# Attention over pairs of heads: two 64-row rotary products in neighbouring PSUM banks, and the causal mask added by VectorE

## The chip, the cores and the metric

The kernel runs on one core of a Trainium2 chip. Its time is the device time of one execution in microseconds (us); the figure to compare is the median over several executions. A profile of one execution, with a record for nearly every instruction, goes with it.

## The reference, cut to what matters

A two-layer decoder trunk over 512 tokens of width 1024, in float32. Layer 0 has a state-space and a gated linear recurrence mixer, layer 1 has multi-head latent attention, and each layer ends in a mixture of experts (64 experts). The change lies in the attention of layer 1 alone:

```
q, k: 8 heads of 192 = 128 ("nope") + 64 (rotary); v: 8 heads of 128
for each block of 128 queries:
    s = einsum('bhqd,bhkd->bhqk', q_blk, k) / sqrt(192)
    s = where(key_pos <= q_pos, s, -1e30)
    p = softmax(s)
    o = einsum('bhqk,bhkd->bhqd', p, v)
x = x + concat(o) @ w_o
```

## The kernel before, in words

The core has five engines with an instruction stream each: TensorE (PE), VectorE (DVE), ScalarE (ACT), GpSimd (POOL) and SyncE (SP), which only issues transfers. Each stream is executed in the order in which the program wrote it; streams wait for each other by semaphores, and nothing but the waits in the code orders them.

The attention (`odd_tensor`, `odd_scalar`, `odd_vector`) goes over 32 units, numbered n = 8c + i: query block c of 4, head i of 8. The kernel is causal, so a unit of block c meets only (c + 1) * 128 keys. Below k stands for c + 1, the number of 128-key pieces, 1 to 4. `ps` is the accumulator memory PSUM, eight banks of 512 float32 per partition. For one unit:

- PE, "QK": `qTn` by `kTn`, 128 rows deep (L923), then the mask added by a product of the identity with the mask matrix on the last 128 columns (L924), then the rotary part `qTr` by `kTr`, 64 rows deep (L925). The rotary parts of two heads lie over one another in the partitions: even heads in partitions 0 to 63, odd heads in 64 to 127. The product ends with an increment of `s_sc`. Scores of unit n go to bank n % 3.
- VectorE: row maximum of the scores (L1094), its multiple as bias (L1097, which increments `s_mx`).
- ScalarE: exponential out of PSUM into `pr` with the row sum (L1016, `s_ex`).
- VectorE: reciprocal of the sum (L1102) and scaling of `pr` (L1104, `s_pn`).
- PE: k transposes of `pr` into banks 3 and 4 (L933, `s_pt`).
- ScalarE: copy of these into `pT` (L1024, `s_pte`).
- PE, "AV": k products of V with `pT` into bank 5 or 6 (L943, `s_o`). After four heads VectorE copies the bank to `oT` (L1109, `s_oe`).

The order on each engine is written out by hand as a software pipeline. PE: QK of n, transposes of n - 2, AV of n - 3. VectorE: maximum and bias of n, then reciprocal and scaling of n - 1. ScalarE: exponential of n, then the copy of n - 2:

```python
for n in range(NHD + 3):          # PE;  NHD = 32
    ...QK(n)...
    m = n - 2
    if 0 <= m < NHD:
        TE.wait_ge(s_pn, m + 1)   # the scaled probabilities of unit m
    ...
for n in range(H * TC + 5):       # VectorE
    if n < H * TC:
        V.wait_ge(s_sc, n + 1)
        vlink(V.reduce_max(...n...)) ...
    m = n - 1
    if 0 <= m < H * TC:
        V.wait_ge(s_ex, m + 1) ... .then_inc(s_pn, 1)
```

`vlink` makes VectorE wait for its own instruction before the next one. Each float32 matmul is recorded as two PE instructions, called passes here; a transpose is one.

Ahead of the attention come the projections and the normalisation of q and k, behind it the output projection (`outproj_tensor`, L441), which waits for the last `oT` copy, then the norm, the routing and the experts. SP waits for `s_sc` of the last unit (L1819) before it loads the first expert weights of layer 1 into the buffers that held q and k.

Of the kernel before, what the change touches and what calls it, by code (L numbers as in the profile page):

```python
# [8 lines left out]
ALU = mybir.AluOpType  # L9
ACT = mybir.ActivationFunctionType  # L10
AX = mybir.AxisListType

P = 128
# [9 lines left out]
H = 8  # L23
QL, KVL, NOPE, ROPE, VD = 384, 256, 128, 64, 128
QK = NOPE + ROPE
MLA_IN = QL + KVL + ROPE
ATT_SCALE = 1.0 / math.sqrt(QK)
# [45 lines left out]
def hybrid_decoder(nc, a, out):  # L73
    ctx = ExitStack()
    with ctx:
# [14 lines left out]
        extra = sb("extra", [P, 4096])  # L90
# [5 lines left out]
        ps = ctx.enter_context(nc.psum_tensor("ps", [P, 8, 512], F32))  # L96

        ident = con[:, C_ID:C_ID + P]
# [3 lines left out]
        mask = con[:, C_MASK:C_MASK + P]  # L102
# [18 lines left out]
        r3 = ring[3][:, :, :].rearrange("p a b -> p (a b)")  # L121
# [25 lines left out]
        def vlink(ins):  # L147
            chain["v"] += 1
            ins.then_inc(s_v, 1)
            nc.vector.wait_ge(s_v, chain["v"])  # L150
# [11 lines left out]
        V, S, G, TE = nc.vector, nc.scalar, nc.gpsimd, nc.tensor  # L162
# [377 lines left out]
        def tt(o, p, q, op):  # L540
            vlink(V.tensor_tensor(o, p, q, op))  # L541
# [251 lines left out]
        vbuf = rega[:, :].rearrange("p (c n) -> p c n", c=TC)  # L793
# [12 lines left out]
        rp = [r[:, 2560:3584].rearrange("p (h d) -> p h d", h=2 * H) for r in rows]  # L806
        sq = extra[:, 0:1536]
        cbuf = extra[:, 1536:1536 + MLA_IN]
        pr = [r3[:, 4096:4608], extra[:, 2240:2752], r3[:, 4608:5120]]
        pT = [extra[:, 2752:3264], extra[:, 3264:3776]]  # L810
        kro = extra[:, 3776:4032].rearrange("p (c d) -> p c d", c=TC)
        half = ROPE // 2
        rt = [sq[:, i * 512:(i + 1) * 512].rearrange("p (h d) -> p h d", h=2 * H) for i in range(3)]
# [52 lines left out]
        def odd_tensor():  # L866
            for n in range(2):
                for c in range(TC):
                    if c == 0:
                        TE.wait_ge(s_win, 32)  # L870
                    for k in range(KC):
                        last = TE.matmul(ps[:, 4 * n + c, 0:HW], hT[:, k, c * P:(c + 1) * P], win[n][:, k, :],  # L872
                                         start=k == 0, stop=k == KC - 1)
                    last.then_inc((s_ch, s_c)[n], 1)
                    if n and c:
                        odd_ctrans(c - 1)
            odd_ctrans(TC - 1)
            for u, (kind, c, n) in enumerate(UNITS):
                if u == 0:
                    TE.wait_ge(s_uq, 16)  # L880
                    TE.wait_ge(s_cte, TC)
                if u == 3:
                    TE.wait_ge(s_ukv, 16)
                if u >= 8:
                    TE.wait_ge(*copied(u - 8))
                bank = ps[:, u % 8, :]
                cc = slice(c * P, (c + 1) * P)
                if kind == "q":
                    for k in range(3):
                        last = TE.matmul(bank, cT[:, k, cc], wuq[:, k, n * 512:(n + 1) * 512],  # L890
                                         start=k == 0, stop=k == 2)
                elif kind == "kv":
                    for k in range(2):
                        last = TE.matmul(bank, cT[:, 3 + k, cc], wukv[:, k, n * 512:(n + 1) * 512],
                                         start=k == 0, stop=k == 1)
                else:
                    if n == 0:
                        TE.wait_ge(s_qn, c + 1)
                    for j in range(4):
                        if n < 2:  # L900
                            src = qi[c % 2][:, 4 * n + j, 0:NOPE]
                        elif n < 4:
                            src = ki[c % 2][:, 4 * (n - 2) + j, :]
                        else:
                            src = rp[c % 2][:, 8 * (n - 4) + 2 * j:8 * (n - 4) + 2 * j + 2, :]\
                                .rearrange("p h d -> p (h d)")
                        last = TE.transpose(bank[:, j * P:(j + 1) * P], src, ident)
                last.then_inc(s_q, 1)
            for u in range(len(UNITS) - 8, len(UNITS)):
                TE.wait_ge(*copied(u))  # L910


            NHD = H * TC
            for n in range(NHD + 3):
                if n < NHD:
                    c, i = n // H, n % H
                    nk = (c + 1) * P
                    if n >= 3:
                        TE.wait_ge(s_ex, n - 2)
                    r = slice(64 * (i % 2), 64 * (i % 2) + 64)  # L920
                    cc = slice(c * P, (c + 1) * P)
                    o = ps[:, n % 3, 0:nk]
                    TE.matmul(o, qTn[:, i, cc], kTn[:, i, 0:nk], start=True, stop=False)  # L923
                    TE.matmul(ps[:, n % 3, nk - P:nk], ident, mask, start=False, stop=False)  # L924
                    TE.matmul(o, qTr[r, i // 2, cc], kTr[r, i // 2, 0:nk], start=False, stop=True)\  # L925
                        .then_inc(s_sc, 1)
                m = n - 2
                if 0 <= m < NHD:
                    TE.wait_ge(s_pn, m + 1)
                    if m >= 2:  # L930
                        TE.wait_ge(s_pte, m - 1)
                    for b in range(m // H + 1):
                        last = TE.transpose(ps[:, 3 + m % 2, b * P:(b + 1) * P],  # L933
                                            pr[m % 3][:, b * P:(b + 1) * P], ident)
                    last.then_inc(s_pt, 1)
                m = n - 3
                if 0 <= m < NHD:
                    c, i = m // H, m % H
                    if m % 4 == 0 and m >= 8:
                        TE.wait_ge(s_oe, m // 4 - 1)  # L940
                    TE.wait_ge(s_pte, m + 1)
                    for b in range(c + 1):
                        last = TE.matmul(ps[:, 5 + (m // 4) % 2, (m % 4) * P:(m % 4 + 1) * P],  # L943
                                         vbuf[:, b, i * VD:(i + 1) * VD],
                                         pT[m % 2][:, b * P:(b + 1) * P], start=b == 0, stop=b == c)
                    last.then_inc(s_o, 1)
            TE.wait_ge(s_oe, 2 * TC)
            outproj_tensor(lambda k, c: oT[:, k, c * P:(c + 1) * P])

# [7 lines left out]
        def odd_scalar():  # L957
# [52 lines left out]
            for n in range(H * TC + 2):  # L1010
                if n < H * TC:
                    nk = (n // H + 1) * P
                    S.wait_ge(s_mx, n + 1)
                    if n >= 3:
                        S.wait_ge(s_pt, n - 2)
                    S.activation(pr[n % 3][:, 0:nk], ps[:, n % 3, 0:nk], ACT.Exp, scale=ATT_SCALE,  # L1016
                                 bias=nb[:, n % 3:n % 3 + 1], accum_out=rs[:, n % 3:n % 3 + 1]).then_inc(s_ex, 1)
                m = n - 2
                if m >= 0:
                    nk = (m // H + 1) * P  # L1020
                    S.wait_ge(s_pt, m + 1)
                    if m >= 2:
                        S.wait_ge(s_o, m - 1)
                    S.activation(pT[m % 2][:, 0:nk], ps[:, 3 + m % 2, 0:nk], ACT.Copy).then_inc(s_pte, 1)  # L1024

        def odd_vector():

# [61 lines left out]
            for n in range(H * TC + 5):  # L1089
                if n < H * TC:  # L1090
                    nk = (n // H + 1) * P
                    b = n % 3
                    V.wait_ge(s_sc, n + 1)
                    vlink(V.reduce_max(mx[:, b:b + 1], ps[:, b, 0:nk], AX.X))  # L1094
                    if n >= 3:
                        V.wait_ge(s_ex, n - 2)
                    V.tensor_scalar(nb[:, b:b + 1], mx[:, b:b + 1], -ATT_SCALE, None, ALU.mult).then_inc(s_mx, 1)  # L1097
                m = n - 1
                if 0 <= m < H * TC:
                    b = m % 3  # L1100
                    V.wait_ge(s_ex, m + 1)
                    vlink(V.reciprocal(ri[:, b:b + 1], rs[:, b:b + 1]))  # L1102
                    nk = (m // H + 1) * P
                    V.tensor_scalar(pr[b][:, 0:nk], pr[b][:, 0:nk], ri[:, b:b + 1], None, ALU.mult).then_inc(s_pn, 1)  # L1104
                if n >= 8 and n % 4 == 0:
                    g = n // 4 - 2
                    V.wait_ge(s_o, 4 * g + 4)
                    c, b = g // 2, g % 2
                    V.tensor_copy(oT[:, 4 * b:4 * b + 4, c * P:(c + 1) * P],  # L1109
                                  ps[:, 5 + g % 2, :].rearrange("p (h t) -> p h t", h=4)).then_inc(s_oe, 1)  # L1110
# [869 lines left out]
```

## Time and profile before

| | |
|---|---|
| median of 3 executions | 1644.01 us (1641.84 to 1645.41) |
| the profiled execution | 1644.24 us |
| its span, first to last instruction | 1642.3 us |
| PE busy in the span | 1351.0 us (82%) |
| VectorE, ScalarE busy | 490.5 us, 287.3 us |
| attention, first QK to first output projection | 944.08 to 1025.28 us |

In the rows of the profile, times are microseconds from the start of the span unless marked ns. "PEld" is a weight load of PE. The busy time of a matmul holds the time of its results through the array, so successive matmuls overlap in the records; what one costs in a dense stretch is read from start to start. A row of a table of stretches gives the stretch, its length, the busy time and instructions of PE, PEld, VectorE, ScalarE and POOL, the granted PE clock as a share of full speed, the busy share of the transfer engines and GB/s.

### The profile page before, as it was taken

Reading aid. Unit: us, or ns where it says so; the run is one execution under the profiler, and the core shown is the slowest. Engines: PE = TensorE matmul, PEld = TensorE weight load, DVE = VectorE, ACT = ScalarE, POOL = GpSimd, SP = SyncE. Lnnn points to the kernel's source line nnn. Section 1 sums busy time; section 2 is a strip of 40 time slices with the busy share of each in tenths; the row PEclk is TensorE's granted clock in tenths of the full one; section 3 lists DMA queues with packets and bytes.
Section 4 is the critical chain, followed back from the end, with each engine's and each line's share of the span. In section 5 each row is a group of like instructions: output and inputs, shape, how many; then the busy total and the mean of one; then the engine's idle time right before and its main releaser. Section 6 shows DMA issues by size and latency. Waiting matters only on the chain.

```text
span 1642.3 us, 19412 instructions
## 1 busy us (share of the span) xinstructions
PE 1351.0 (82%) x6152; PEld 632.2 (38%) x6152; DVE 490.5 (30%) x940; ACT 287.3 (17%) x564; POOL 316.6 (19%) x427
## 2 busy tenths in 40 slices
PE   5988995988777878788889699977988787878786
PEld 4555453333223333333544376453333232333332
DVE  6996125111111111112507654142111111111114
ACT  3235110111001010101243443111111000010100
POOL 6213001232221212121000000002332222212220
PEclk9999996999999998989889799988999999999988
DMA  6514724999999999997220301366999999999995
GB/s 210 211 46 151 298 97 160 394 387 406 402 402 399 405 395 413 401 399 290 99 109 1 116 1 63 142 256 247 393 401 401 392 402 394 409 404 403 389 382 235
DMA packets 83522, 472.36 MB, mean 288 GB/s; under 512 B 13970, under 2 KB 16194, under 8 KB 32912
## 3 DMA queue, kind: packets, MB, share of 16 engines
q1 hardware_dynamic: 69792, 445.25, 68.7%
q0 software_dynamic: 11952, 20.14, 3.8%
q10 hardware_dynamic: 1728, 6.29, 0.9%
q8 instruction: 33, 0.54, 0.1%
q14 instruction: 17, 0.14, 0.0%
HBM read 454.59 MB, written 27.39 MB: 293 GB/s over the span
## 4 chain that ended last, share of the span: by engine, by line
PE 43%; SPq 31%; DVE 13%; issue 6%; DMA 5%; ACT 2%; DVEq 0%; POOL 0%; ACTq 0%; POOLq 0%
SPq L1600 20%; PE ps L1395 14%; SPq L1605 11%; PE ps L1415 6%; DMA ring<-in_moe_w 4%; PE ps L441 3%; PE ps L1385 2%; PE ps L872 2%; PE ps L315 2%; PE ps L390 2%; PE ps L430 2%; DVE ring L541 1%; PE ps L925 1%; PE ps L943 1%; DVE extra L541 1%
## 5 line engine op out<-in xcount | busy, mean ns | idle before, releaser
L1395 PE MATMUL ps<-ring,region_b 128*64 128x512 f32 x1408 | 342.3, 642 | 79.7 <-issue 53.7
L1395 PEld LDWEIGHTS ps<-ring,region_b 128*64 128x64 f32 x1408 | 116.3, 148 | 303.1 <-issue 265.7
L1532 DVE TENSOR_TENSOR extra<-extra,ps 128x256 f32<-128x256 f32 x64 | 27.0, 421 | 609.5 <-ACT extra L1470 609.5
L1395 PE MATMUL ps<-wbuf,region_b 128*64 128x512 f32 x320 | 165.6, 678 | 48.3 <-DMA region_a<-in_moe_w 29.1
L1415 PE MATMUL ps<-ring,extra 128*64 128x512 f32 x704 | 160.8, 598 | 34.2 <-DVE extra L1538 34.2
L1395 PE MATMUL ps<-region_a,region_b 128*64 128x512 f32 x320 | 165.8, 678 | 0.0
L1339 POOL DMA_INDIRECT region_b<-hrow,icol x120 | 111.2, 927 | 148.2 <-issue 148.2
L1351 POOL DMA_INDIRECT ytok<-extra,icol x120 | 105.6, 880 | 154.1 <-issue 154.1
L1470 ACT ACTIVATE extra<-ps 128x256 f32<-128x256 f32 x64 | 24.6, 384 | 593.0 <-PE ps L1395 593.0
L1545 DVE COPY extra<-ps 128x512 f32<-128x512 f32 x64 | 44.3, 692 | 242.2 <-PE ps L1415 242.2
L1395 PEld LDWEIGHTS ps<-wbuf,region_b 128*64 128x64 f32 x320 | 48.2, 156 | 160.6 <-issue 150.1
L1415 PEld LDWEIGHTS ps<-ring,extra 128*64 128x64 f32 x704 | 49.8, 136 | 114.8 <-issue 89.7
L1349 POOL COPY icol<-blkidx 64x2 int32 x60 | 10.5, 175 | 421.4 <-DVE extra L1545 421.4
L1385 PEld LDWEIGHTS ps<-con,region_b 128*128 128x128 f32 x512 | 63.2, 195 | 64.3 <-issue 64.3
L1385 PE MATMUL ps<-con,region_b 128*128 128x128 f32 x512 | 75.7, 292 | 13.6 <-DMA region_b<-hrow,blkidx 13.6
L1415 PE MATMUL ps<-wbuf,extra 128*64 128x512 f32 x320 | 73.1, 597 | 16.7 <-DVE extra L1538 16.7
L1476 ACT ACTIVATE extra<-ps 128x512 f32<-128x512 f32 x64 | 38.2, 597 | 276.1 <-PE ps L1415 276.1
L315 PE MATMUL ps<-region_b,wbuf 128*128 128x512 f32 x128 | 55.8, 594 | 0.0
L1463 ACT ACTIVATE region_b<-ps 128x512 f32<-128x512 f32 x64 | 38.2, 597 | 81.5 <-PE ps L1385 81.5
L1839 POOL DMA_DIRECT2D gain<-in_p_norms x4 | 2.4, 600 | 252.1 <-DVEq L1088 168.7
L1527 DVE COPY region_b<-ps 128x512 f32<-128x512 f32 x64 | 44.3, 692 | 18.5 <-PE ps L1385 18.3
L1395 PEld LDWEIGHTS ps<-region_a,region_b 128*64 128x64 f32 x320 | 48.1, 156 | 0.0
(297 smaller groups left out, 1568.6 us busy)
## 6 DMA issues: line engine op xcount, KB each, us to landing
ring<-in_moe_w SPq DMA_DIRECT2D x264, 1024.0 KB, 26.3
wbuf<-in_moe_w SPq DMA_DIRECT2D x80, 1024.0 KB
region_a<-in_moe_w SPq DMA_DIRECT2D x40, 1024.0 KB
ytok<-ring SPq DMA_DIRECT2D x8, 1024.0 KB, 10.2
wbuf<-in_ev_w_in SPq DMA_DIRECT2D x3, 2048.0 KB, 17.2
wbuf<-in_ev_w_out SPq DMA_DIRECT2D x2, 2048.0 KB, 14.2
hrow<-region_a ACTq DMA_DIRECT2D x8, 512.0 KB, 10.8
region_a<-ytok SPq DMA_DIRECT2D x8, 512.0 KB, 5.3
```

The source lines that it names most:

```text
L315: last = TE.matmul(ps[:, bank, :], w[:, k, m * P:(m + 1) * P], hT[:, k, :], start=k == 0, stop=k == KC - 1)
L441: last = TE.matmul(ps[:, 4 + (n + 2) % 4, :], lhs(k, n // 2), wout[n % 2][:, k, :], start=k == 0, stop=k == KC - 1)
L1339: G.indirect_dma_start(xin[j][CAP * g:CAP * g + n, :], None, hrow[l], bass.IndirectOffsetOnAxis(ap=icol[0:n, 2 * j + g:2 * j + g + 1], axi ...
L1351: G.indirect_dma_start(ytok[l], bass.IndirectOffsetOnAxis(ap=icol[0:n, 4 + 2 * j + g:5 + 2 * j + g], axis=0), yo[j][CAP * g:CAP * g + n, : ...
L1385: last = TE.transpose(ps[:, k // 4, (k % 4) * PAIR:(k % 4 + 1) * PAIR], xin_block(j, k), ident)
L1395: last = TE.matmul(ps[CAP * g:CAP * (g + 1), 2 + j, :], xtr[j][:, k, CAP * g:CAP * (g + 1)], up_weights(2 * slot + g, k), start=k == 0, st ...
L1415: last = TE.matmul(ps[CAP * g:CAP * (g + 1), 6 + nh, :], hidT[j][:, f, CAP * g:CAP * (g + 1)], w2[2 * slot + g][:, f * D + nh * 512:f * D ...
L1463: S.activation(xtr[j][:, 4:8, :].rearrange("p k s -> p (k s)"), ps[:, 1, :], ACT.Copy)\
L1527: V.tensor_copy(xtr[j][:, 0:4, :].rearrange("p k s -> p (k s)"), ps[:, 0, :])\
L1545: V.tensor_copy(yo[j][:, 0:512], ps[:, 6, :]).then_inc(ml["s_ye"][l], 1)
L1600: nc.sync.dma_start(w13[b][:, n, :], src).then_inc(s, 16)
L1605: nc.sync.dma_start(w2[b], src).then_inc(s, 16)
```

## The change

PE works in steps of two units (2g and 2g + 1): the 128-row products of both, then the 64-row products of both, one next to the other in the program, one in partitions 0 to 63 and one in 64 to 127, into two different banks. Then come the transposes of 2g - 2 and 2g - 1, then AV of 2g - 4 and 2g - 3. The identity product for the mask is gone from PE; VectorE adds the mask to the last 128 columns of the scores in PSUM, in place, before the row maximum. Scores have four banks (0, 1, 2, 7), `pr` four buffers and `pT` three, and the waits for free buffers follow. The order of VectorE's and ScalarE's streams stays.

```diff
@@ -806,8 +806,9 @@
         rp = [r[:, 2560:3584].rearrange("p (h d) -> p h d", h=2 * H) for r in rows]
         sq = extra[:, 0:1536]
         cbuf = extra[:, 1536:1536 + MLA_IN]
-        pr = [r3[:, 4096:4608], extra[:, 2240:2752], r3[:, 4608:5120]]
-        pT = [extra[:, 2752:3264], extra[:, 3264:3776]]
+        pr = [r3[:, 4096 + i * 512:4608 + i * 512] for i in range(4)]
+        pT = [extra[:, 2240 + i * 512:2752 + i * 512] for i in range(3)]
+        SBANK = (0, 1, 2, 7)
         kro = extra[:, 3776:4032].rearrange("p (c d) -> p c d", c=TC)
         half = ROPE // 2
         rt = [sq[:, i * 512:(i + 1) * 512].rearrange("p (h d) -> p h d", h=2 * H) for i in range(3)]
@@ -911,39 +912,40 @@
 
 
             NHD = H * TC
-            for n in range(NHD + 3):
-                if n < NHD:
-                    c, i = n // H, n % H
+            for g in range(NHD // 2 + 2):
+                if g < NHD // 2:
+                    c = 2 * g // H
                     nk = (c + 1) * P
-                    if n >= 3:
-                        TE.wait_ge(s_ex, n - 2)
-                    r = slice(64 * (i % 2), 64 * (i % 2) + 64)
                     cc = slice(c * P, (c + 1) * P)
-                    o = ps[:, n % 3, 0:nk]
-                    TE.matmul(o, qTn[:, i, cc], kTn[:, i, 0:nk], start=True, stop=False)
-                    TE.matmul(ps[:, n % 3, nk - P:nk], ident, mask, start=False, stop=False)
-                    TE.matmul(o, qTr[r, i // 2, cc], kTr[r, i // 2, 0:nk], start=False, stop=True)\
-                        .then_inc(s_sc, 1)
-                m = n - 2
-                if 0 <= m < NHD:
-                    TE.wait_ge(s_pn, m + 1)
-                    if m >= 2:
-                        TE.wait_ge(s_pte, m - 1)
-                    for b in range(m // H + 1):
-                        last = TE.transpose(ps[:, 3 + m % 2, b * P:(b + 1) * P],
-                                            pr[m % 3][:, b * P:(b + 1) * P], ident)
-                    last.then_inc(s_pt, 1)
-                m = n - 3
-                if 0 <= m < NHD:
-                    c, i = m // H, m % H
-                    if m % 4 == 0 and m >= 8:
-                        TE.wait_ge(s_oe, m // 4 - 1)
-                    TE.wait_ge(s_pte, m + 1)
-                    for b in range(c + 1):
-                        last = TE.matmul(ps[:, 5 + (m // 4) % 2, (m % 4) * P:(m % 4 + 1) * P],
-                                         vbuf[:, b, i * VD:(i + 1) * VD],
-                                         pT[m % 2][:, b * P:(b + 1) * P], start=b == 0, stop=b == c)
-                    last.then_inc(s_o, 1)
+                    for n in (2 * g, 2 * g + 1):
+                        if n >= 4:
+                            TE.wait_ge(s_ex, n - 3)
+                        TE.matmul(ps[:, SBANK[n % 4], 0:nk], qTn[:, n % H, cc], kTn[:, n % H, 0:nk],
+                                  start=True, stop=False)
+                    for n in (2 * g, 2 * g + 1):
+                        r = slice(64 * (n % 2), 64 * (n % 2) + 64)
+                        TE.matmul(ps[:, SBANK[n % 4], 0:nk], qTr[r, n % H // 2, cc], kTr[r, n % H // 2, 0:nk],
+                                  start=False, stop=True).then_inc(s_sc, 1)
+                for m in (2 * g - 2, 2 * g - 1):
+                    if 0 <= m < NHD:
+                        TE.wait_ge(s_pn, m + 1)
+                        if m >= 2:
+                            TE.wait_ge(s_pte, m - 1)
+                        for b in range(m // H + 1):
+                            last = TE.transpose(ps[:, 3 + m % 2, b * P:(b + 1) * P],
+                                                pr[m % 4][:, b * P:(b + 1) * P], ident)
+                        last.then_inc(s_pt, 1)
+                for m in (2 * g - 4, 2 * g - 3):
+                    if m >= 0:
+                        c, i = m // H, m % H
+                        if m % 4 == 0 and m >= 8:
+                            TE.wait_ge(s_oe, m // 4 - 1)
+                        TE.wait_ge(s_pte, m + 1)
+                        for b in range(c + 1):
+                            last = TE.matmul(ps[:, 5 + (m // 4) % 2, (m % 4) * P:(m % 4 + 1) * P],
+                                             vbuf[:, b, i * VD:(i + 1) * VD],
+                                             pT[m % 3][:, b * P:(b + 1) * P], start=b == 0, stop=b == c)
+                        last.then_inc(s_o, 1)
             TE.wait_ge(s_oe, 2 * TC)
             outproj_tensor(lambda k, c: oT[:, k, c * P:(c + 1) * P])
 
@@ -1011,17 +1013,17 @@
                 if n < H * TC:
                     nk = (n // H + 1) * P
                     S.wait_ge(s_mx, n + 1)
-                    if n >= 3:
-                        S.wait_ge(s_pt, n - 2)
-                    S.activation(pr[n % 3][:, 0:nk], ps[:, n % 3, 0:nk], ACT.Exp, scale=ATT_SCALE,
+                    if n >= 4:
+                        S.wait_ge(s_pt, n - 3)
+                    S.activation(pr[n % 4][:, 0:nk], ps[:, SBANK[n % 4], 0:nk], ACT.Exp, scale=ATT_SCALE,
                                  bias=nb[:, n % 3:n % 3 + 1], accum_out=rs[:, n % 3:n % 3 + 1]).then_inc(s_ex, 1)
                 m = n - 2
                 if m >= 0:
                     nk = (m // H + 1) * P
                     S.wait_ge(s_pt, m + 1)
-                    if m >= 2:
-                        S.wait_ge(s_o, m - 1)
-                    S.activation(pT[m % 2][:, 0:nk], ps[:, 3 + m % 2, 0:nk], ACT.Copy).then_inc(s_pte, 1)
+                    if m >= 3:
+                        S.wait_ge(s_o, m - 2)
+                    S.activation(pT[m % 3][:, 0:nk], ps[:, 3 + m % 2, 0:nk], ACT.Copy).then_inc(s_pte, 1)
 
         def odd_vector():
 
@@ -1091,7 +1093,9 @@
                     nk = (n // H + 1) * P
                     b = n % 3
                     V.wait_ge(s_sc, n + 1)
-                    vlink(V.reduce_max(mx[:, b:b + 1], ps[:, b, 0:nk], AX.X))
+                    bank = ps[:, SBANK[n % 4], :]
+                    tt(bank[:, nk - P:nk], bank[:, nk - P:nk], mask, ALU.add)
+                    vlink(V.reduce_max(mx[:, b:b + 1], bank[:, 0:nk], AX.X))
                     if n >= 3:
                         V.wait_ge(s_ex, n - 2)
                     V.tensor_scalar(nb[:, b:b + 1], mx[:, b:b + 1], -ATT_SCALE, None, ALU.mult).then_inc(s_mx, 1)
@@ -1101,7 +1105,8 @@
                     V.wait_ge(s_ex, m + 1)
                     vlink(V.reciprocal(ri[:, b:b + 1], rs[:, b:b + 1]))
                     nk = (m // H + 1) * P
-                    V.tensor_scalar(pr[b][:, 0:nk], pr[b][:, 0:nk], ri[:, b:b + 1], None, ALU.mult).then_inc(s_pn, 1)
+                    V.tensor_scalar(pr[m % 4][:, 0:nk], pr[m % 4][:, 0:nk], ri[:, b:b + 1], None, ALU.mult)\
+                        .then_inc(s_pn, 1)
                 if n >= 8 and n % 4 == 0:
                     g = n // 4 - 2
                     V.wait_ge(s_o, 4 * g + 4)
```

## Rows read from the trace of the kernel before

**Rows 1.** The page: span, and each engine's busy time, share and instructions.

```profile
span 1642.3 us, 19412 instructions
...
PE 1351.0 (82%) x6152; PEld 632.2 (38%) x6152; DVE 490.5 (30%) x940; ACT 287.3 (17%) x564; POOL 316.6 (19%) x427
```

**Rows 2.** Busy time by query block, k = 1 to 4.

```profile
944.08:954.23 10.15, 10.15 (x65) 8.18 (x65) 5.55 (x27) 5.21 (x20) 0.00 (x0) 1.00 0.00 1
954.23:970.12 15.89, 15.89 (x91) 11.86 (x89) 9.26 (x37) 6.29 (x24) 0.00 (x0) 1.00 0.00 1
970.12:992.08 21.96, 21.96 (x115) 14.51 (x114) 10.84 (x36) 8.17 (x25) 0.00 (x0) 1.00 0.00 1
992.08:1025.28 33.20, 32.28 (x170) 20.80 (x169) 14.61 (x39) 12.00 (x29) 0.00 (x0) 1.00 0.17 64
```

**Rows 3.** Who waited for whom from 944 to 1026 us: total, times, longest.

```profile
DVE smalls L1094 <- PE ps L925: 42.0, 32, 7.5
...
PEld ps L933 <- DVE ring L1104: 0.3, 1, 0.3
```

**Rows 4.** PE in time order at k = 4: start, duration, line, shapes.

```profile
1007.88 0.66 PE L933 MATMUL ps<-con,ring 128*128 128x128 f32 x4
1008.37 1.06 PE L943 MATMUL ps<-extra,region_a 128*128 128x128 f32 x8
1009.26 1.02 PE L923 MATMUL ps<-ring 128*128 128x512 f32 x2
1010.12 0.38 PE L924 MATMUL ps<-con 128*128 128x128 f32 x2
1010.44 1.12 PE L925 MATMUL ps<-ring 64*128 64x512 f32 x2
1011.49 0.66 PE L933 MATMUL ps<-con,ring 128*128 128x128 f32 x4
```

**Rows 5.** PE in time order at k = 1.

```profile
948.85 0.39 PE L923 MATMUL ps<-ring 128*128 128x128 f32 x2
...
949.39 0.49 PE L925 MATMUL ps<-ring 64*128 64x128 f32 x2
949.81 0.33 PE L933 MATMUL ps<-con,ring 128*128 128x128 f32 x1
...
950.20 0.39 PE L923 MATMUL ps<-ring 128*128 128x128 f32 x2
```

**Rows 6.** VectorE in time order at k = 4, one unit.

```profile
1015.21 0.69 DVE L1094 TENSOR_REDUCE smalls<-ps 128x1 f32<-128x512 f32 x1 [2.14 <-PE ps L925]
1015.94 0.15 DVE L1097 TENSOR_SCALAR smalls<-smalls 128x1 f32<-128x1 f32 x1
1016.01 0.15 DVE L1102 RECIPROCAL smalls<-smalls 128x1 f32<-128x1 f32 x1
1016.20 0.49 DVE L1104 TENSOR_SCALAR ring<-ring,smalls 128x512 f32<-128x512 f32 x1
```

**Rows 7.** All engines around 1020 us, at the end of attention.

```profile
1019.81 0.49 DVE L1104 TENSOR_SCALAR ring<-ring,smalls 128x512 f32<-128x512 f32 x1
...
1020.35 0.42 PEld L933 LDWEIGHTS ps<-con,ring 128*128 128x128 f32 x4 [0.28 <-DVE ring L1104]
```

**Rows 8.** VectorE groups by shape: busy us, mean ns of one.

```profile
L1094 DVE TENSOR_REDUCE smalls<-ps 128x1 f32<-128x128 f32 x8 | 2.3, 292 | 10.5 <-PE ps L925 10.5
...
L541 DVE TENSOR_TENSOR extra<-ps,extra 128x256 f32<-128x256 f32 x4 | 1.7, 424 | 0.1
...
L1104 DVE TENSOR_SCALAR ring<-ring,smalls 128x128 f32<-128x128 f32 x5 | 1.4, 288 | 0.2
```

**Rows 9.** PE at the 64-row, 64-column gate products of layer 0.

```profile
104.30 1.93 PE L374 MATMUL ps<-ring 64*64 64x512 f32 x8
```

**Rows 10.** Stretches ahead of and behind the attention: clock and transfers.

```profile
926.00:943.20 17.20, 5.25 (x24) 4.98 (x24) 10.44 (x15) 7.48 (x15) 0.54 (x1) 0.50 0.51 183
1040.00:1080.00 40.00, 40.00 (x95) 17.76 (x94) 7.54 (x12) 5.61 (x10) 0.00 (x0) 1.00 0.01 2
```

## The prediction

> **What bounds the kernel now.** The page comes first: PE is busy for 82% of the span, VectorE for 30% [rows 1]. A share over the whole span says little of one stage, so the attention is cut out by query block. It takes 81.2 us (944.08 to 1025.28), PE is busy in all but 0.9 us of it, VectorE in 40.3 us [rows 2]. The waits of this stretch say the same from the other side: VectorE waits 32 times for PE's score products, 42 us in all, while PE waited only once for the scaled probabilities, 0.3 us, at the very end [rows 3]. So PE sets the pace, and the next view is PE in order of time.
>
> At k = 4 a unit takes 3.61 us (L933 at 1007.88 to L933 at 1011.49). Start to start: 4 transposes 0.49, 8 AV passes 0.89, 2 QK passes 0.86, 2 mask passes 0.32, 2 rotary passes 1.05 [rows 4]. A 512-column pass thus costs 0.43 and a 128-column AV pass 0.11. By the same rate the mask would be 0.22 and the rotary part 0.86: there are 0.10 us ahead of the 64-row products and 0.19 at them that no column explains, and at the transposes another 0.05 over 4 times 0.11. The same excess is there at k = 1, where the rotary part takes 0.42 for 0.21 of columns [rows 5]. So going from full depth to 64 rows costs about 0.2 us (the pipe empties, and the first weight load is not hidden) and coming back about 0.15. A unit at k = 1 takes 1.35 us [rows 5]; between the two, size and time go in proportion.
>
> **The change part by part: what PE saves.** The mask product: 32 units by 0.22 = 7.0 us. The change of shape, once per pair in place of once per unit: 16 by 0.35 = 5.6 us. The rotary products side by side: 4 passes of a pair in the time of 2. This core has done it with 64-row products already, though with 64 columns of weights: 8 passes of 512 columns took 1.93 us [rows 9], where 8 times 0.43 is 3.4. Over the four sizes (passes of 0.11, 0.21, 0.32, 0.43, four pairs each) that saves 8 by 1.07 = 8.5 us. Together 21.1 us, if PE stays the bound.
>
> The Trainium skill has the same picture: its page "TensorEngine Tiling (Array Packing)", section Key Properties, says that tiles work independently and in parallel, and that changing the tiling mode drains the engine. The trace agrees with the drain (the 0.10 us above). By this page alone the change is worth about the whole 21 us, which is the first rival below.
>
> **What it costs.** VectorE gains an add on 128 columns with one operand and the result in PSUM, per unit. No row has the result in PSUM. The nearest: an add with one operand from PSUM takes 0.42 for 256 columns; a row maximum of 128 columns out of PSUM takes 0.29, a scaling of 128 in SBUF 0.29 [rows 8]. A maximum goes from 0.29 at 128 columns to 0.69 at 512 [rows 6, 8], 0.13 per 128, so 0.42 for 256 is 0.29 for 128. I take 0.29. Below it stands 0.22: the 0.15 of an instruction on one column plus 0.07, the scaling's growth per 128 columns (0.29 to 0.49 over three of them) [rows 6, 8]. Above it stands 0.45, somewhat over the 256-column time, since a write to PSUM is in no row. `vlink` adds the gap 0.03 (1015.21 + 0.69 to 1015.94).
>
> Where it lies matters more. Before, PE transposed unit n - 2 after QK of n, and VectorE delivers `s_pn` of n - 2 right behind the maximum of n - 1, so PE never waited. Now PE finishes QK of 2g and 2g + 1 and then wants the probabilities of 2g - 1. But VectorE's stream has the scaling of 2g - 1 behind the mask and maximum of 2g, whose scores PE has just finished. So in each pair PE waits for a whole VectorE chain at its transposes of 2g - 1. Queued behind that wait on PE are the AV products of 2g - 4 and 2g - 3 and then QK of the next pair, none of which needs it; behind them wait VectorE, ScalarE and, at the end, the output projection.
>
> The chain, from the last rotary column: to VectorE 0.20 (before, the maximum starts 0.10 behind the transposes, which themselves come 0.10 behind the last column), add and gap 0.32, maximum and gap 0.73 at k = 4, bias to reciprocal 0.07, to scaling 0.19, scaling 0.49 [rows 6], to PE 0.05 (1019.81 + 0.49 to 1020.35) [rows 7], first transpose 0.05: 2.1 us at k = 4, and 0.92 + 0.29 + 0.29 = 1.5 at k = 1. PE's transposes of 2g - 2 fit inside (0.6). The rest is a stall: 1.5 us a pair at k = 4, 1.2 at k = 1, where before was none.
>
> **The sum over the stage**, in the order of PE's path: 64 QK passes, 16 of each size, 16 by 1.08 = 17.3; into the 64-row shape, 16 by 0.2 = 3.2; two rotary slots per pair 8.5; the chain 15 times: fixed part 15 by 0.92 = 13.8, maxima of the even units 2 to 30 (0.29, 0.43, 0.56, 0.69, four each but one at k = 1) 7.6, scalings of the odd units 1 to 29 (0.29, 0.35, 0.42, 0.49) 5.7; transposes of those odd units, 36 by 0.11 = 4.0; AV of units 0 to 27, 64 pieces of two passes by 0.223 = 14.3. Then the tail: 8 transposes 0.9, AV of four units 3.6, the last `oT` copy and the way to the projection 1.0. And at the start VectorE, with the first two units on hand at once, comes about 0.85 late to the second pair, and PE leaves the first pair's shape for 0.15. In all 80.9 us, against 81.2. The 21 us are saved and given back as stalls: PE's own work would be some 60 us.
>
> Three edits cost nothing here. The third `pT`, the fourth `pr` and the fourth bank relax waits (for exponentials three or more units back) that took no time before and take none now; without them PE would wait for ScalarE as well. Whether the rotary products really overlap changes nothing either: if they ran one after the other, `s_sc` of the even unit would still come after two slots, and the chain starts there; the 0.86 us of the odd unit would lie inside the 1.5 us stall.
>
> Behind the attention everything moves along: the output projection waits for the last copy. SP's first expert weights, released by the last QK, start some 3 us earlier relative to the projection, which is worth nothing, as their buffers are full long before: no traffic from 1040 to 1080 [rows 10].
>
> The profiled execution took 1644.24 us, 1.9 over its span and 0.2 over the median; against the median, 81.2 to 80.9 makes 1643.7 us. A difference under 0.2% (3.3 us) can't be told from none in this kernel.
>
> **Rivals.** First, bound by PE and faster: if PE were not held by that chain, the stage would fall to about 60 us, 1623 us. For it: PE's saving is in the rows, and VectorE has time (40 of 81 us, plus 32 by 0.32 = 10). Against it: the program order, which no queue on PE passes. Chance 0.05.
>
> Second, a shorter chain: an add of 0.22 takes 15 by 0.07 off and a little at the start, 1642.5; to leave the 0.2% it would need 0.2 us off each of the 15 rounds, which several hand-overs at once would have to give. Faster by over 0.2% along this way: 0.07. The case that the add alone is cheap stays in the forecast.
>
> Third, a dear add: at 0.45 each round is 0.16 longer and VectorE later at the start, in all 2.8 us: 1646.5; it decides from about 0.49, for which a PSUM write dearer than every PSUM read of the rows would be needed. Chance 0.11 for slower by over 0.2%, at about 1649.
>
> Fourth, the clock. The granted clock was at half (1.2 GHz) from 926 to 943.2, where PE was busy 5.25 of 17.2 us [rows 10], and full (2.4 GHz) in all four blocks, where PE never paused [rows 2]. With stalls of 1.2 us in pairs of 2.9 us the first block is no longer dense. At half clock PE's exposed work there (0.44 + 0.2 + 0.21 + 0.11 + 0.45 = 1.4 us) doubles: 4 pairs by 1.4 = 5.6 us, 1649; it decides from three such pairs on. Against it: the pauses are short, and PE still works half of the time. Chance 0.10.
>
> **How the numbers follow.** Forecast 0.67 (within 0.2%), first rival 0.05, second 0.07, third 0.11, fourth 0.10. Faster 0.12, same 0.67, slower 0.21. The likeliest case by itself spans 1642 to 1647 (add of 0.22 to 0.45). The range takes in the clock: 1640 to 1649.5.
>
> **What would show it.** In the profile after: no identity products with the mask; PE waiting for VectorE's scaling (L1108) some 15 times, about 1.2 to 1.5 us each, 20 us in all; pairs of 2.9, 4.3, 5.7 and 7.1 us; an add of about 0.29; rotary products of a pair with equal starts. Wrong would be: PE without such waits; an add over 0.45; a clock of 0.5 after 944; an attention stage under 78 or over 84 us.

## The result, and the profile after

The changed kernel takes 1649.61 us, the median of 8 executions (1647.32 to 1651.8), against 1643.88 us before (8 executions, 1641.84 to 1646.17): a ratio of 1.0035, 95% interval 1.0025 to 1.0046. It is slower by about 5.7 us. Forecast was 1643.7, range 1640.0 to 1649.5, with 0.21 for slower.

The page of the changed kernel's profile, against [rows 1]:

```profile
span 1648.1 us, 19314 instructions
...
PE 1346.8 (82%) x6088; PEld 626.6 (38%) x6088; DVE 497.4 (30%) x972; ACT 287.2 (17%) x564; POOL 316.0 (19%) x427
```

The span is 5.8 us longer, though PE is busy less. The attention by query block, against [rows 2] (columns as there, the clock third from the right):

```profile
945.50:957.55 12.05, 8.40 (x47) 6.49 (x47) 8.09 (x38) 5.62 (x23) 0.00 (x0) 0.76 0.01 2
957.55:976.70 19.15, 14.75 (x71) 9.68 (x71) 11.08 (x42) 6.18 (x24) 0.00 (x0) 0.80 0.00 1
976.70:998.50 21.80, 16.90 (x97) 10.53 (x95) 12.85 (x43) 8.41 (x27) 0.00 (x0) 1.00 0.00 0
998.50:1031.28 32.78, 26.73 (x161) 17.61 (x159) 16.30 (x46) 11.39 (x27) 0.00 (x0) 1.00 0.27 103
```

It takes 85.8 us (945.50 to 1031.28) where it took 81.2. Ahead of it 1.4 us were lost, in code that the change doesn't touch; the start of the attention lay anywhere from 944.1 to 947.9 us in the fourteen profiles of this study, so that part is scatter. Behind it 616.8 us against 617.0: nothing. PE, which had paused for 0.9 us in all, is now busy for 66.8 of 85.8 us, and its clock was 0.76 and 0.80 of full speed in the first two blocks. The waits of the stage, against [rows 3]:

```profile
DVE ps L541 <- PE ps L927: 36.4, 15, 7.5
PEld ps L935 <- DVE ring L1108: 22.0, 16, 1.6
PE ps L935 <- DVE ring L1108: 18.2, 16, 1.4
```

PE waits 16 times for the scaled probabilities, 18.2 us (22.0 counted on its weight loads). The chain of work that ended last, for one round at k = 4 (start, duration, engine and line; pieces under 0.2 us left out), shows the loop:

```profile
1005.16 1.72 PE ps L923 x4
1006.88 1.11 PE ps L927 x4
1007.98 0.29 DVE ps L541
...
1008.30 0.70 DVE smalls L1098
...
1009.28 0.50 DVE ring L1108
...
1009.83 0.66 PE ps L935 x4
1010.48 1.34 PE ps L945 x12
1011.82 1.72 PE ps L923 x4
```

From QK of one pair at 1005.16 to that of the next at 1011.82 it is 6.7 us: 2.8 on PE, then 1.8 in which PE's next step stands behind VectorE's add, maximum and scaling, then transposes and AV. Two things of PE can be read in order of time, with [rows 4] and [rows 7] for comparison:

```profile
1006.80 1.13 PE L927 MATMUL ps<-ring 64*128 64x512 f32 x4
1007.86 0.42 PEld L935 LDWEIGHTS ps<-con,ring 128*128 128x128 f32 x4 [0.76 <-issue]
...
1007.97 0.30 DVE L541 TENSOR_TENSOR ps<-ps,con 128x128 f32<-128x128 f32 x1 [2.45 <-PE ps L927]
1008.30 0.69 DVE L1098 TENSOR_REDUCE smalls<-ps 128x1 f32<-128x512 f32 x1
...
1009.28 0.49 DVE L1108 TENSOR_SCALAR ring<-ring,smalls 128x512 f32<-128x512 f32 x1
...
1009.82 0.42 PEld L935 LDWEIGHTS ps<-con,ring 128*128 128x128 f32 x4 [1.54 <-DVE ring L1108]
```

The four rotary passes of a pair take 1.06 us (1006.80 to the next weight load at 1007.86); before, the two of one unit took 1.05 [rows 4]. So they do run side by side. And PE waits 1.5 us for L1108. The add, 32 times, against [rows 8]:

```profile
L541 DVE TENSOR_TENSOR ps<-ps,con 128x128 f32<-128x128 f32 x32 | 9.4, 295 | 36.4 <-PE ps L927 36.4
```

What the forecast left out of its likeliest case (it is the fourth rival there, with a chance of 0.10) is a fall of the clock. The stretches in which it changed, for the changed kernel:

```profile
944.80:951.70 6.90, 3.96 (x27) 2.81 (x27) 4.45 (x22) 4.00 (x12) 0.00 (x0) 0.99 0.01 2
951.70:965.30 13.60, 11.17 (x39) 7.83 (x41) 6.68 (x29) 3.96 (x18) 0.00 (x0) 0.50 0.00 1
965.30:979.00 13.70, 10.32 (x61) 6.50 (x61) 8.13 (x31) 5.03 (x18) 0.00 (x0) 1.00 0.01 1
```

and for the kernel before, where it stayed full:

```profile
944.80:951.70 6.90, 6.90 (x44) 5.53 (x45) 4.07 (x21) 3.24 (x14) 0.00 (x0) 1.00 0.00 0
951.70:965.30 13.60, 13.60 (x78) 10.10 (x77) 8.15 (x33) 5.86 (x24) 0.00 (x0) 1.00 0.01 2
```

It rose to full (2.4 GHz) about when the attention starts in both, after some 17 us at half [rows 10]. In the changed kernel it fell to half (1.2 GHz) again at 951.7 us, for 13.6 us.

### The profile page after: what moved, and what is told of

The parts are those of the page before. It is cut to its first block, busy times and chain, and to the rows that moved or that the text cites. A ratio compares the mean times of both kernels' runs of the same rounds, so it can differ in the third digit from the quotient of the medians.

```text
span 1648.1 us, 19314 instructions
## 1 busy us (share of the span) xinstructions
PE 1346.8 (82%) x6088; PEld 626.6 (38%) x6088; DVE 497.4 (30%) x972; ACT 287.2 (17%) x564; POOL 316.0 (19%) x427
## 3 DMA queue, kind: packets, MB, share of 16 engines
q1 hardware_dynamic: 69792, 445.25, 68.3%
## 4 chain that ended last, share of the span: by engine, by line
PE 41%; SPq 31%; DVE 14%; issue 6%; DMA 5%; ACT 2%; DVEq 0%; POOL 0%; POOLq 0%; ACTq 0%
SPq L1605 20%; PE ps L1400 13%; SPq L1610 10%; PE ps L1420 6%; DMA ring<-in_moe_w 4%; PE ps L441 3%; PE ps L873 2%; PE ps L315 2%; PE ps L390 2%; PE ps L430 2%; PE ps L1390 2%; DVE ring L541 1%; PE ps L923 1%; PE ps L945 1%; DVE extra L541 1%
## 5 line engine op out<-in xcount | busy, mean ns | idle before, releaser
L1400 PE MATMUL ps<-ring,region_b 128*64 128x512 f32 x1408 | 346.5, 649 | 75.1 <-issue 52.0
```

Source lines behind the costliest of these rows:

```text
L1400: last = TE.matmul(ps[CAP * g:CAP * (g + 1), 2 + j, :], xtr[j][:, k, CAP * g:CAP * (g + 1)], up_weights(2 * slot + g, k), start=k == 0, st ...
```

## The experiments

A plain sum over PE's, VectorE's and ScalarE's streams, with the durations and hand-overs of the rows and each wait of the code, carries the forecast's arithmetic through all 32 units. The stage times that the expectations name come from it. Every ratio below is to the kernel before, run alongside on the same chip.

**e1: work in the stalls.** Edit to the changed kernel:

```diff
                         if m >= 2:
                             TE.wait_ge(s_pte, m - 1)
+                        if m == 2 * g - 1 and g < H:
+                            for _ in range(4):
+                                TE.matmul(ps[:, 4, 384:512], ident, mask, start=True, stop=True)
+                        TE.wait_ge(s_pn, m + 1)
```

(the wait for `s_pn` moves behind the extra products)

> The changed kernel with 4 extra identity products of 128 columns (8 passes, 0.9 us at full clock) on PE, put into the wait for the scaled probabilities of the odd unit, in the pairs of the first two query blocks only; their result is overwritten unused. Clock theory: of the 4.6 us by which the attention stage grew (81.2 to 85.8), nearly all is the clock that fell to half (1.2 GHz) at 951.7 us for 13.7 us; PE that works through its stalls keeps the full clock, the products fit inside the 1.2 us stalls, and the stage falls back to about 81 us although 6 us of work were added: total 1645 us, 4 to 5 below the changed kernel. Rival, that the stalls or VectorE's add alone make the loss and the clock is no part of it: the same time as the changed kernel (1649.6) or longer, up to 1656 if the products don't fit.

Measured: 1643.95 us, ratio to the kernel before 1.000 (0.999 to 1.001). The stage took 81.6 us at full clock, in these stretches of its trace:

```profile
944.80:951.70 6.90, 5.17 (x39) 3.82 (x37) 4.00 (x19) 4.27 (x13) 0.00 (x0) 0.97 0.01 2
951.70:965.30 13.60, 12.95 (x90) 10.02 (x89) 9.65 (x41) 5.64 (x24) 0.00 (x0) 1.00 0.00 1
965.30:979.00 13.70, 11.89 (x76) 8.32 (x72) 9.06 (x32) 5.24 (x18) 0.00 (x0) 1.00 0.00 1
```

The kernel has more PE work, put into waits, so nothing on the path got shorter. Yet the stage takes 4.2 us less, and the kernel, 5.7 us over the kernel before as changed, is 0.8 over it here: the clock theory holds. It also shows the changed order at full clock: about 81 us, as the forecast's sum had it.

**e2: products in turn.** Edit to the changed kernel:

```diff
                         TE.matmul(ps[:, SBANK[n % 4], 0:nk], qTn[:, n % H, cc], kTn[:, n % H, 0:nk],
                                   start=True, stop=False)
-                    for n in (2 * g, 2 * g + 1):
                         r = slice(64 * (n % 2), 64 * (n % 2) + 64)
                         TE.matmul(ps[:, SBANK[n % 4], 0:nk], qTr[r, n % H // 2, cc], kTr[r, n % H // 2, 0:nk],
                                   start=False, stop=True).then_inc(s_sc, 1)
```

> The changed kernel with the products of a pair in the old order (128-row and 64-row products of the even unit, then those of the odd one), everything else as changed: nothing lies side by side any more and PE changes its shape twice as often. Theory of the chain: the scores of the even unit come earlier by the odd unit's products, VectorE's chain runs beside them, and the stall nearly goes; the same arithmetic that gave 80.9 us gives 75.4 us for the stage, so 1638 us (up to 1642 if the clock still falls). Rival, that the side-by-side placement is worth its saved passes (8.5 us) and saved shape changes (5.6 us): longer than the changed kernel, 1655 to 1663 us.

Measured: 1647.79 us, ratio 1.0032 (1.0021 to 1.0043), stage 84.9 us: neither theory's number. The trace tells why:

```profile
948.50:972.40 23.90, 23.90 (x69) 15.39 (x68) 12.76 (x54) 7.99 (x32) 0.00 (x0) 0.50 0.00 0
972.40:1030.90 58.50, 57.74 (x289) 34.35 (x288) 35.17 (x109) 23.84 (x62) 0.00 (x0) 1.00 0.12 48
```

The clock was at half for 23.9 us. The waits of PE for the scaled probabilities were down to 7, 4.0 us in all, from 16 and 22.0 on the weight loads:

```profile
PEld ps L934 <- DVE ring L1107: 4.0, 7, 0.8
```

From the ninth pair on, at full clock, a pair took 4.65 to 6.83 us against 5.10 to 7.11 in the changed kernel, 0.3 to 0.45 us less in each. The chain theory, with 75.4 for 80.9 us, had 5.5 us less over 16 pairs, 0.34 each, although nothing runs side by side.

**e3: AV first.** On PE, with the two loops of each step written as functions of the unit, `transposes` and `weighted` (AV):

```diff
-transposes(2 * g - 2); transposes(2 * g - 1); weighted(2 * g - 4); weighted(2 * g - 3)
+transposes(2 * g - 2); weighted(2 * g - 4); weighted(2 * g - 3); transposes(2 * g - 1)
```

> The changed kernel with one reordering on PE: transposes of 2g - 2, then AV of 2g - 4 and 2g - 3, then the transposes of 2g - 1 (before, both AV came behind them). AV work of 0.45 us (k = 1) to 1.8 us (k = 4) fills the wait. Theory of the chain: stage 68 us at full clock, stalls left only at k = 1 and 2; 1631 us, or 1634 if the clock falls again in the first block. Rival, that VectorE's own work with the added mask (or the add in PSUM) bounds the stage: no gain over the changed kernel, 1645 us or more.

Measured: 1634.09 us, ratio 0.9939 (0.9926 to 0.9952). Stage 70.5 us with 6.8 us at half clock. Of the 18.2 us that PE waited for the scaled probabilities, 5.3 are left:

```profile
PE ps L935 <- DVE ring L1112: 5.3, 10, 1.0
```

The chain theory holds, and with the clock's part it gives this number: the rival, VectorE as the bound of the changed kernel, is out.

**e4: the mask alone.** Edit to the kernel before:

```diff
-                    TE.matmul(ps[:, n % 3, nk - P:nk], ident, mask, start=False, stop=False)
...
+                    tt(ps[:, b, nk - P:nk], ps[:, b, nk - P:nk], mask, ALU.add)
                     vlink(V.reduce_max(mx[:, b:b + 1], ps[:, b, 0:nk], AX.X))
```

> The kernel before with the mask part alone: no identity product on PE, VectorE adds the mask in PSUM ahead of the maximum; units one by one, three score banks as before. Theory of the chain: here the maximum of unit n is one unit off the transposes, VectorE's add of 0.29 us is hidden from k = 2 on, and the stage falls from 81.2 to 76.4 us: 1639 us. Rival, that the add is what made the changed kernel slower: no gain, 1644 us or more.

Measured: 1648.06 us, ratio 1.0033 (1.0015 to 1.005), stage 85.3 us: a miss, and taken alone it would have spoken for the rival. Its trace:

```profile
944.40:946.90 2.50, 2.50 (x12) 1.73 (x12) 1.45 (x7) 1.60 (x3) 0.00 (x0) 1.00 0.00 0
946.90:970.80 23.90, 23.43 (x72) 15.31 (x71) 12.76 (x54) 7.36 (x32) 0.00 (x0) 0.50 0.00 0
970.80:1029.70 58.90, 57.67 (x287) 33.88 (x286) 35.56 (x109) 22.69 (x62) 0.00 (x0) 1.00 0.10 39
```

Half clock for 23.9 us again. It set in before PE had waited for VectorE at all: the first such wait ends at 947.39 us. In the last block, at full clock, a pair of units takes 6.79 us, the 7.23 of before less two mask products of 0.22. The add costs nothing there.

**e12: the mask moved from the third block on.** As e4, but with the product kept for `n < 16` and the add used for `n >= 16`.

> The kernel before, unit by unit, with the mask moved to VectorE only from the third block on (units 16 to 31). PE's stream in the first two blocks is that of the kernel before, with which the clock was full. Theory: 16 products of 0.22 us go, VectorE's add is hidden: stage 81.2 to 77.7 us, clock full, 1640.4 us. Rival, that taking work off PE anywhere costs the clock as in e4: 1644 us or more.

Measured: 1641.92 us, ratio 0.9986 (0.9977 to 0.9995), stage 78.0 us, full clock throughout. The saving is 3.2 us in the stage, where 3.5 was expected; over all it is 2 us. Together with e4: moving the mask is a small gain, and what it cost in e4 was the clock.

**e9: the mask part undone in the changed kernel.** `ident` by `mask` behind each QK product again, no add on VectorE.

> The changed kernel with the mask part undone: identity products on PE again, no add on VectorE, pairs and side-by-side products as changed. Theory of the chain: each round loses VectorE's add (0.32 us) and gains two mask products (0.44 us) on PE, both on the path, so at full clock the stage is 82.1 us, slightly longer than the 81 of the changed order; what decides is the clock: the stalls shrink from 1.25 to 0.93 us at k = 1 with the same work around them plus 0.44 us, so PE is denser, the clock holds, 1645 us. Rival, that the add in PSUM is what costs: stage 76 to 78 us, 1640 us. Second rival, the clock falls as in the changed kernel: 86 us, 1649 us.

Measured: 1644.11 us, ratio 1.0003 (0.9992 to 1.0013), stage 82.4 us, clock full. PE still waits 15 times for VectorE, 12.7 us. So the pairs with side-by-side products alone gain nothing, with or without the mask part, and with the product in place the clock holds.

**e5 and e6: fillers for e2 and e3.** Two extra products per pair in the first two blocks for e2's order, four in the first block for e3's.

> The kernel of e2 (products of a pair in turn) with 2 extra identity products (4 passes, 0.44 us) on PE ahead of the wait for the odd unit's scaled probabilities, in the pairs of the first two query blocks. e2 had the short periods of the chain theory where the clock was full (5.3 to 6.8 us from k = 3 on) and lost 9 us to a half clock of 23.9 us. If the clock is the whole of that miss and the filler holds it, the stage is 76.6 us: 1639 us. Rival, that the clock falls anyway since the gaps stay: 85 us, 1648 us as e2.

> The kernel of e3 (AV ahead of the odd unit's transposes) with 4 extra identity products (8 passes, 0.9 us) at the same place, in the pairs of the first query block only. e3 took 70.4 us with 6.8 us at half clock. Clock theory: full clock throughout, stage 68.3 us, 1632 us against 1634. Rival, that the clock falls later all the same or the fillers lengthen the path: 70 us or more, 1634 to 1636.

e5: 1646.94 us, ratio 1.0016 (1.0007 to 1.0024), stage 83.2 us with 13.7 us at half clock. That is a miss (1639 expected), but not a test of whether the filler holds the clock: the clock fell at 950.4 us, before the first extra product (L934) at 952.1:

```profile
950.40:964.10 13.70, 13.70 (x50) 10.80 (x49) 6.99 (x33) 4.88 (x20) 0.00 (x0) 0.50 0.00 1
952.09 1.06 PE L934 MATMUL ps<-con 128*128 128x128 f32 x4
```

In e1 the first extra product ran at 949.3 us, while the clock was still full. The time at half is shorter in e5 than in e2, 13.7 against 23.9 us; that the fillers did this is likely and not shown.

e6: 1633.18 us, ratio 0.9928 (0.9913 to 0.9943), stage 69.3 us at full clock, where 68.3 was expected; the difference to e3 in time is not clear of the scatter.

**e7 and e10: VectorE's stream in pairs as well.** On top of e3, with four columns for maxima and sums:

```diff
-for n: maximum(n); scaled(n - 1)
+for n in steps of 2: maximum(n); maximum(n + 1); scaled(n); scaled(n + 1)
```

e7 has two extra products per pair in the first two blocks, e10 none.

> e3 with VectorE's stream in pairs too (mask and maximum of 2g and 2g + 1, then scaling of 2g and 2g + 1, with four buffers for the row sums), so that the odd unit's scaling no longer stands behind the next pair's maximum, and 2 extra identity products per pair in the first two blocks. Theory of the chain: PE-bound from k = 3 on, stage 64.9 us: 1628 us, the fastest of all. Rival, that VectorE's load (about 50 us of work, and both scalings behind both maxima) bounds it: no better than e3, 1634 us.

> e7 without the extra identity products. At full clock the stage would be 64.0 us, 0.9 less than with them. Clock theory: the gaps of the first block (0.7 us in 2.4 us periods) are about those of e3, where the clock fell for 6.8 us and cost 2.5 us: stage 66 to 67 us, 1630 us, that is 1 to 2 above e7. Rival, that the clock holds without them: 64 us, 1627.5 us.

e7: 1628.77 us, ratio 0.990 (0.9885 to 0.9915), stage 65.3. e10: 1628.22 us, ratio 0.9903 (0.9886 to 0.9919), stage 64.3. In both the clock was full, in e10 against the expectation, with this first block:

```profile
946.40:958.00 11.60, 9.10 (x62) 6.82 (x63) 9.11 (x42) 5.79 (x23) 0.00 (x0) 1.00 0.01 2
```

**e8: the price of side by side.** e7 with the products in turn, by the edit of e2.

> e7 with the products of a pair in turn in place of side by side: the price of the side-by-side products where PE sets the pace. Theory: 8.5 us of passes and 16 changes of shape of 0.35 us (5.6 us) come back where PE is the bound, less what VectorE's pace hides in the first blocks: stage 76 us, 11 us over e7: 1639 us. Rival, that the two rows of products share a limit and give little: within 3 us of e7.

Measured: 1645.74 us, ratio 1.0014 (1.0004 to 1.0024): 17 us over e7. The stage took 80.2 us against 65.3, with 6.8 us at half clock; the fall came at 950.1 us, again before the first extra product (950.9). The stage is 4 us over the 76 expected, of which the half clock can explain up to 3.4 (half of its length); the rest is open. The price is read where both have the full clock. From the first pair of the second block to the output projection e8 takes 67.7 us and e7 56.0. The 11.7 us between them fit the forecast's prices, which give 7.7 for the passes and 4.2 for 12 changes of shape there. At k = 4, PE in order of time for e8:

```profile
1015.08 1.02 PE L923 MATMUL ps<-ring 128*128 128x512 f32 x2
1016.04 1.12 PE L926 MATMUL ps<-ring 64*128 64x512 f32 x2
1017.09 1.12 PE L923 MATMUL ps<-ring 128*128 128x512 f32 x2
1018.15 1.12 PE L926 MATMUL ps<-ring 64*128 64x512 f32 x2
1019.20 0.66 PE L937 MATMUL ps<-con,ring 128*128 128x128 f32 x4
```

and for e7:

```profile
995.64 1.88 PE L923 MATMUL ps<-ring 128*128 128x512 f32 x4
997.45 1.13 PE L927 MATMUL ps<-ring 64*128 64x512 f32 x4
998.51 0.66 PE L938 MATMUL ps<-con,ring 128*128 128x128 f32 x4
```

From the first QK product to the transposes, e7 takes 2.87 us (995.64 to 998.51). In e8 the four parts take 0.96, 1.05, 1.06 and 1.05: 4.12 us (1015.08 to 1019.20). The 1.25 us between them are two passes of 0.43 and one change of shape of 0.39, where the forecast had 0.86 + 0.35. The rival is out.

**e11: useful work for filler.** e10 with the mask as a product for `n < 16`, on VectorE from there.

> e7 with useful work in place of the extra products: for the units of the first two blocks the mask stays an identity product on PE, from the third block on VectorE adds it. PE is dense (0.9 us of gaps in the whole stage) and VectorE's chain shorter in the blocks where it sets the pace: clock full, stage 63.4 us, 1627 us, the fastest. Rival, that side-by-side products and dense QK in the first block still let the clock fall as in e2, e4, e5 and e8: 67 us or more, 1631 us.

Measured: 1628.13 us, ratio 0.9907 (0.9892 to 0.9922), stage 63.7 us, clock full. By its stage the shortest, in time level with e7 and e10; all three beat both kernels by about 1%.

The stage of every profile, with the time at half clock in it, and beside it the granted clock over the whole kernel (share of full speed), the mean of all its executions:

| kernel | stage us | half clock us | median us | clock, all executions |
|---|---|---|---|---|
| before | 81.2 | 0 | 1643.9 | 0.926 |
| changed | 85.8 | 13.6 | 1649.6 | 0.924 |
| e1 changed, filler | 81.6 | 0 | 1644.0 | 0.927 |
| e9 changed, mask on PE | 82.4 | 0 | 1644.1 | 0.928 |
| e2 in turn | 84.9 | 23.9 | 1647.8 | 0.919 |
| e5 in turn, filler | 83.2 | 13.7 | 1646.9 | 0.923 |
| e4 before, mask on VectorE | 85.3 | 23.9 | 1648.1 | 0.920 |
| e12 mask late | 78.0 | 0 | 1641.9 | 0.926 |
| e3 AV first | 70.5 | 6.8 | 1634.1 | 0.925 |
| e6 AV first, filler | 69.3 | 0 | 1633.2 | 0.927 |
| e8 both orders, in turn | 80.2 | 6.8 | 1645.7 | 0.924 |
| e7 both orders, filler | 65.3 | 0 | 1628.8 | 0.926 |
| e10 both orders | 64.3 | 0 | 1628.2 | 0.927 |
| e11 both orders, mask split | 63.7 | 0 | 1628.1 | 0.926 |

The last column shows that the falls are no accident of the profiled executions: the six kernels with a fall in the profile average 0.925 at most, the eight without one 0.926 at least, though single executions overlap (0.921 to 0.926 changed, 0.922 to 0.930 before). In the seven experiments whose clock stayed full (e1, e6, e7, e9 to e12) the measured stage lies 0.3 to 1.0 us over the sum that was expected.

## Why the prediction was wrong, point by point

- **PE's savings**: right. The mask products are gone, the rotary passes of a pair run side by side (e7 against e8), the shape changes once per pair. 1.25 us a pair at k = 4 measured, 1.21 forecast. The page "TensorEngine Tiling (Array Packing)" of the Trainium skill, section Key Properties, says that tiles work in parallel and that a change of mode drains the engine. The runs agree: four passes of a pair in 1.06 us, and 0.39 us for one change of shape there and back. The saving is the kernel's only where PE is not kept waiting (e7, e10).
- **VectorE's add**: right, 0.29 to 0.30 us, as long as the scaling of 128 columns within SBUF, 0.29 [rows 8]. The third rival is out.
- **The new wait**: right in place and size. 16 waits, 18.2 us, against some 15 and 20; 1.5 us at k = 4. e3 moves nothing but AV, PE's wait falls from 18.2 to 5.3 us and the stage from 85.8 to 70.5; with VectorE's stream in pairs too, the wait is 3.9 us in e10.
- **The sum at full clock**: right. 80.9 forecast; e1, whose extra products lie inside stalls, took 81.6. The first rival, which ends at the 60 us of PE's own work, names what another order comes near to: e10 takes 64.3.
- **The step that failed**: "the pauses are short, and PE still works half of the time", by which the fourth rival got a chance of 0.10 and the forecast a clock that stays full. The premise held, PE was busy for 3.96 of the 6.90 us ahead of the fall, but the inference did not: the clock fell at 951.7 us for 13.6 us. That rival's mechanism is what happened, and its 1649 us is within 1 us of the median. Its placing was off: it priced four pairs of the first block at 1.4 us. The clock fell only in the third pair and stayed down into the second block, where a pair has more work: against e1, the pairs from 949.9 to 968.1 us took 0.5, 1.3, 1.9 and 1.0 us longer, 4.7 us in all. That is the loss of the stage (4.6 us), a little under the 5.6 of that rival. The median rose by 5.7 us. Where the other 1.1 us come from no run tells; the start of the attention, outside the change, scatters by more. The range ended 0.1 us below the median.
- **The mask part alone** fails at the same step: by the same arithmetic the stage of e4 should have gained 5 us, and it lost 4. The clock took the 9 us between them; where it was full, e4 ran as the arithmetic has it.
- **The third `pT`, the fourth `pr` and the fourth bank**, and what the stage would be if the rotary products did not overlap: no run tested these two statements.
- **The earlier weight loads** of the experts: worth nothing, as forecast; 616.8 against 617.0 us behind the attention.

Open is what makes the clock fall. It is not the share of time that the records show PE busy: it fell in e4 with PE busy 2.50 of 2.50 us, and held in e10 with 9.1 of 11.6 us. Nor is it how soon after the rise of the clock the attention starts: that is 0.4 to 1.0 us in all fourteen profiles, after 17 us at half, and each of the six falls came 3.4 to 6.9 us after that rise. A warm-up ahead of the attention was not tried. Fillers kept the clock in e1 (against the changed kernel) and e6 (against e3). In e5 and e8 they came too late to tell, and e10 kept the clock without those of e7.

## What to carry to other kernels

When two units are issued as a pair, look at who waits for the first one's result: side-by-side products delay the even unit's scores until the odd one's are done, and every engine's stream must be moved by the same step, or the saving of 21 us turns into waits of the same size. With PE as the bound, work taken off it in a stage that begins at a freshly risen clock can cost more than it saves, as in e4; compare stage times at equal clock before an operation is judged, since e4 alone would have condemned an add that costs nothing. Moving both streams gave most of the saving, 16.9 (e10) and 17.5 us (e11) of the stage where 21 were forecast for PE, and kept the clock too.

## What the runs showed of the hardware that was not expected

- Taking 0.22 us of product per unit off a dense PE (e4) let the clock fall from 946.9 to 970.8 us, though PE's records show no pause between the first QK product (944.4) and the fall. The only one just ahead is the 0.8 us before that product, which the kernel before has as well. The full clock came back 1 us after the third block had begun (969.8), with no change in the order.
- Adding 28 products whose result nobody uses, in 7 of the 18 steps, made the kernel about 5 us faster, each measured against the kernel before (5.7 and 0.8 us over it; e1).
- The Trainium skill's page "TensorE: Matmul & The Clock Gate", section Loop structure matters more than you think, says that the loop nest decides whether the clock stays up, and blames long waits of PE for transfers. The runs agree that what stands in the stream decides (e9 to e11 against e2 to e5). They show falls without any long wait as well: PE's longest pause ahead of the fall of e4 is 0.8 us, while e10 has 2.5 us of pauses in 11.6 and keeps the clock.
